# Norm products ordered by sum, the samples' last sum moved to POOL and ACT's queue, the last prompt tile finished in two column halves

## What is computed

```python
    g_, u_ = jnp.split(f @ w_gate_up, 2, axis=-1)
    x = x + rmsnorm((jax.nn.silu(g_) * u_) @ w_down, g_ffn_post)

def rmsnorm(x, g):
    x32 = x.astype(jnp.float32)
    y = x32 * lax.rsqrt(jnp.mean(x32 * x32, axis=-1, keepdims=True) + RMS_EPS)
    return (y * g.astype(jnp.float32)).astype(x.dtype)
```

## Time and profile before

| what | value |
| --- | --- |
| three runs | 806.24, 808.50, 808.62 us; median 808.5 us |
| profiled execution, its own time | 807.31 us |
| span of that execution (first to last instruction) | 805.5 us |
| PE busy | 777.1 us, 96% of the span |
| DVE busy | 472.3 us, 59% |
| ACT busy | 358.1 us, 44% |
| POOL busy | 62.4 us, 8% |
| last product of the down projection starts | 796.04 us after the span's start |
| last store started by SP | 802.93 us |
| mean granted TensorE clock | 0.987 of 2.4 GHz |

### The profile page before, as it was taken

One profiled execution on the slowest core, in us unless ns is written; L12 is line 12 of the kernel. 1 busy time (PEld: TensorE's weight loads), 2 busy tenths in 40 slices (PEclk: granted clock), 3 DMA queues, 4 the chain that ended last, 5 costly groups with the idle time before them and its releaser, 6 DMA issues.

```text
span 805.5 us, 16337 instructions
## 1 busy us (share of the span) xinstructions
PE 777.1 (96%) x6019; PEld 736.3 (91%) x6019; DVE 472.3 (59%) x739; ACT 358.1 (44%) x614; POOL 62.4 (8%) x142
## 2 busy tenths in 40 slices
PE   3999999999999999999999899999999999999996
PEld 2879998999898899996889899999999999999996
DVE  5556646636646643675558877777777776222223
ACT  6235534534534541333465455555555565222222
POOL 3321102011010110004000000000000010000000
PEclk9899999999999999999999999999999999999998
DMA  6654335335422122635443233333333224323222
GB/s 205 176 165 134 101 117 142 91 97 146 126 75 83 52 80 72 218 105 167 148 132 104 56 101 105 104 104 104 104 103 96 61 96 135 99 72 91 78 65 111
DMA packets 148746, 89.09 MB, mean 111 GB/s; under 512 B 8594, under 2 KB 142186, under 8 KB 148715
## 3 DMA queue, kind: packets, MB, share of 16 engines
q1 hardware_dynamic: 146014, 81.63, 34.4%
q0 software_dynamic: 2384, 6.40, 2.3%
q10 hardware_dynamic: 316, 0.66, 0.3%
HBM read 81.85 MB, written 6.81 MB: 110 GB/s over the span
## 4 chain that ended last, share of the span: by engine, by line
PE 91%; DVE 1%; ACT 1%; issue 1%; DVEq 0%; ACTq 0%
PE ps L843 32%; PE ps L1158 25%; PE ps L1223 17%; PE ps L1057 6%; PE ps L1127 3%; PE ps L932 1%; PE ps L945 1%; PE ps L962 1%; PE ps L1004 1%; PE ps L907 1%; PE ps L918 1%; PE ps L975 1%; PE ps L1065 0%; PE ps L1092 0%; PE ps L991 0%
## 5 line engine op out<-in xcount | busy, mean ns | idle before, releaser
L1762 DVE TENSOR_TENSOR w_lo<-w_raw,w_hi 128x1024 fp32r<-128x1024 f32 (+1 forms) x68 | 80.9, 1191 | 141.5 <-ACT w_hi L1300 141.2
L1300 ACT ACTIVATE w_hi<-w_raw 128x1024 fp32r<-128x1024 f32 (+1 forms) x68 | 70.0, 1031 | 142.2 <-PE ps L1223 82.6
L843 PE MATMUL ps<-xin_hi,w_hi 128*128 128x272 f32 x576 | 126.9, 302 | 0.0
L843 PE MATMUL ps<-xin_hi,w_lo 128*128 128x272 f32 x576 | 119.5, 289 | 0.0
L843 PE MATMUL ps<-xin_lo,w_hi 128*128 128x272 f32 x576 | 119.4, 289 | 0.0
L843 PEld LDWEIGHTS ps<-xin_hi,w_hi 128*128 128x128 f32 x576 | 90.6, 190 | 8.9 <-issue 7.6
L843 PEld LDWEIGHTS ps<-xin_lo,w_hi 128*128 128x128 f32 x576 | 91.0, 189 | 0.0
L843 PEld LDWEIGHTS ps<-xin_hi,w_lo 128*128 128x128 f32 x576 | 90.6, 190 | 0.0
L1223 PE MATMUL ps<-hid_hi,w_hi 128*128 128x272 f32 x352 | 76.0, 291 | 0.4 <-DVE hid_lo L2140 0.4
L1223 PE MATMUL ps<-hid_lo,w_hi 128*128 128x272 f32 x352 | 75.0, 287 | 0.0
L1223 PE MATMUL ps<-hid_hi,w_lo 128*128 128x272 f32 x352 | 74.9, 288 | 0.0
(11 more groups left out here) (335 smaller groups left out, 1753.5 us busy)
## 6 DMA issues: line engine op xcount, KB each, us to landing
w_raw<-in_w_in_dram SPq DMA_DIRECT2D x72, 256.0 KB, 3.2
g_raw<-in_w_gate_up_dram SPq DMA_DIRECT2D x40, 256.0 KB, 3.9
w_raw<-in_w_down_dram SPq DMA_DIRECT2D x40, 256.0 KB, 2.9
u_raw<-in_w_gate_up_dram SPq DMA_DIRECT2D x20, 256.0 KB, 3.0
e_raw<-in_w_gate_up_dram SPq DMA_DIRECT2D x20, 256.0 KB, 4.4
kc<-in_cache_k_dram SPq DMA_DIRECT2D x64, 64.0 KB, 1.9
vc<-in_cache_v_dram SPq DMA_DIRECT2D x64, 64.0 KB, 2.0
wo_raw<-in_w_out_dram SPq DMA_DIRECT2D x12, 256.0 KB, 4.0
```

The source lines that it names most:

```text
L843: mm = e.matmul(ps[:, bank + h, 0:HT], wt[:, kw, :], xt[:, kx, h * HT:h * HT + HT], start=first and wt is wh and xt is xh, stop=last and ( ...
L1300: e.activation((to or w_hi[s])[:, 0:k, :], w_raw[s][:, 0:k, :], ACT.Copy).then_inc(hi_done, count)
L1762: e.tensor_tensor(wl[:, 0:k, :], w_raw[s][:, 0:k, :], wh[:, 0:k, :].bitcast(F32), ALU.subtract).then_inc(lo_done, count)
```

## The change

There are four parts.

1. `norm_part` takes the sums in another order. Before, each tile's `yacc` product was followed by its `ysq` product, all behind the wait for the square. Now the `yacc` products of all tiles of the half are made first, without waiting for the square, and then the wait and the `ysq` products. As several sums are open at once, they go to different PSUM banks (6 and 7, and 2 for the samples), and the second half first waits for `y_root` of the first. ACT's roots read from the new places.
2. The samples' last step moves from DVE to POOL, as two instructions (`tensor_scalar`, then `tensor_tensor`, with a semaphore `zs_done` between them). POOL waits for `y_inv` 2 and `yt_free` KD + 2, the same two that DVE waits for.
3. The samples' store moves from SP's queue to ACT's, behind `zs_done` 2, after all that ACT computes.
4. DVE and SP treat prompt tile 3 in two halves of 512 columns: two instructions and two stores of 256 KB, in place of one instruction and one store of 512 KB.

The semaphore `acc_zero` is replaced by one more count of `consts_v`.

```diff
-            for tt in range(TT + 1):
+            for tt in range(TT - 1):
                 e.wait_ge(z_done, tt + 1)
-                if tt < TT:
-                    e.dma_start(y_prompt[0, tt * P:(tt + 1) * P, :], ytok[:, tt, :]).then_inc(y_out, 16)
-                else:
-                    e.dma_start(y_sample.rearrange("b t d -> (b t) d"), ytok[0:TS, TT, :]).then_inc(y_out, 16)
+                e.dma_start(y_prompt[0, tt * P:(tt + 1) * P, :], ytok[:, tt, :]).then_inc(y_out, 16)
+            for c in range(2):
+                cols = slice(NHALF * c, NHALF * c + NHALF)
+                e.wait_ge(z_done, TT + c)
+                e.dma_start(y_prompt[0, SEQ - P:SEQ, cols], ytok[:, TT - 1, cols]).then_inc(y_out, 16)
...
-            e.wait_ge(y_out, 16 * (TT + 1))
+            e.wait_ge(y_out, 16 * (TT + 2))
...
+            e.wait_ge(x1_back, 16 * (TT + 1))
+            e.wait_ge(y_inv, 2)
+            e.wait_ge(yt_free, KD + 2)
+            e.tensor_scalar(ytok[0:TS, TT, :], ytok[0:TS, TT, :], ycol[0:TS, 8 + TT:9 + TT], None, ALU.mult).then_inc(zs_done, 1)
+            e.wait_ge(zs_done, 1)
+            e.tensor_tensor(ytok[0:TS, TT, :], ytok[0:TS, TT, :], x1tok[0:TS, TT, :], ALU.add).then_inc(zs_done, 1)
...
-            def norm_part(tts):
-                for tt in tts:
-                    rows = P if tt < TT else TS
-                    for sums in (yacc, ysq):
-                        mm = e.matmul(ps[0:rows, D_BANK[0], tt:tt + 1], y_cols(sums[:, :], tt), ones[:, 0:1],
+            def norm_part(h):
+
+                units = ((0, 6), (1, 7)) if h == 0 else ((2, 6), (3, 7), (TT, 2))
+                if h == 1:
+                    e.wait_ge(y_root, 1)
+                for sums in (yacc, ysq):
+                    if sums is ysq:
+                        e.wait_ge(y_sq_last, h + 1)
+                    for tt, bank in units:
+                        rows = P if tt < TT else TS
+                        mm = e.matmul(ps[0:rows, bank, h:h + 1], y_cols(sums[:, :], tt), ones[:, 0:1],
                                       start=sums is yacc, stop=sums is ysq)
...
             e.wait_ge(ysq_used, KD)
-            e.wait_ge(y_sq_last, 1)
-            norm_part((0, 1))
+            norm_part(0)
             half_T(0)
             down_steps(2, 1, range(DOWN_K[2]), False, True, hs=(1,)).then_inc(tile_done, 1)
-            e.wait_ge(y_sq_last, 2)
-            norm_part((2, 3, TT))
+            norm_part(1)
             half_T(1)
...
+            e.wait_ge(zs_done, 2)
+            e.dma_start(y_sample.rearrange("b t d -> (b t) d"), ytok[0:TS, TT, :]).then_inc(y_out, 16)
...
-                for tt in (0, 1) if h == 0 else (2, 3, TT):
-                    rows = slice(0, P if tt < TT else TS)
-                    e.scalar_tensor_tensor(ytok[rows, tt, :], ytok[rows, tt, :], ycol[rows, 8 + tt:9 + tt], x1tok[rows, tt, :],
-                                           ALU.mult, ALU.add).then_inc(z_done, 1)
+                for tt in (2 * h, 2 * h + 1):
+                    for cols in (slice(0, D),) if tt < 3 else (slice(0, NHALF), slice(NHALF, D)):
+                        e.scalar_tensor_tensor(ytok[:, tt, cols], ytok[:, tt, cols], ycol[:, 8 + tt:9 + tt], x1tok[:, tt, cols],
+                                               ALU.mult, ALU.add).then_inc(z_done, 1)
```

More of the change, by code:

```diff
@@ L449, in program @@
         ysq_used = sem("ysq_used")
-        acc_zero = sem("acc_zero")
         yt_ready = sem("yt_ready")
@@ L456, in program @@
         z_done = sem("z_done")
+        zs_done = sem("zs_done")
         y_out = sem("y_out")
@@ L1700, in y_roots @@
                 tts = slice(2 * h, 2 * h + 2)
-                last = e.activation(ycol[:, tts], ps[:, 6, tts], ACT.Sqrt, bias=eps_col[:, :], scale=1.0 / D)
+                last = e.activation(ycol[:, tts], ps[:, 6:8, h], ACT.Sqrt, bias=eps_col[:, :], scale=1.0 / D)
                 if h == 1:
-                    last = e.activation(ycol[0:TS, TT:TT + 1], ps[0:TS, 6, TT:TT + 1], ACT.Sqrt, bias=eps_col[0:TS, :],
+                    last = e.activation(ycol[0:TS, TT:TT + 1], ps[0:TS, 2, 1:2], ACT.Sqrt, bias=eps_col[0:TS, :],
                                         scale=1.0 / D)
@@ L2211, in _ @@
             e.wait_ge(q3_done, NS)
-            e.memset(yacc[:, :], 0.0).then_inc(acc_zero, 1)
-            e.wait_ge(acc_zero, 1)
+            e.memset(yacc[:, :], 0.0).then_inc(consts_v, 1)
+            e.wait_ge(consts_v, 4)
             def down_lo(n, odd, c):
```

## The result

The changed kernel is slower by a little. Eight runs have a median of 810.20 us (808.43 to 811.41), eight of the kernel before 807.52 (806.24 to 808.62); the ratio is 1.0037, 95% interval 1.0026 to 1.0047, so about 3.0 us (the two medians differ by 2.7). The forecast was +1.9 us and 809.8 us.

The account below looks back on a forecast made before the run. PE, busy 96% of the span, bounds the kernel, so only the end can move: norm 0.60 us earlier, but POOL's samples work behind DVE's sums gives +1.9 us on 807.9, 809.8 us; range 806.6 to 811.5.

Parts of the forecast that it names:

- DVE's first sum of half 1: Second half's final sums after the norm: DVE's first would start 0.60 us earlier, at 798.64.
- POOL's multiplication: Samples' `tensor_scalar` at the end: 1.12 us for 1024 columns, ending at 802.12 behind DVE's sums.
- Norm products: Second half's norm on PE: `yacc` products hidden ahead of the square, everything behind them 0.60 us earlier.
- Tile 3 in halves: Last prompt tile on DVE and SP: 0.61 us per further half; the prompt's path alone would end 1.0 us earlier.
- The addition: Samples' `tensor_tensor` on POOL after the multiplication: 2.47 us, ending at 804.72.
- the hop: Gap between POOL's two samples instructions: 0.13 us, from 0.08 to 0.18.
- The port: Shared SBUF port at the end: DVE's 2.50 us and POOL's 3.7 us run one behind the other.
- The end: Close of the program: samples' store lands at 806.90, the span ends 0.5 us later at 807.4.
- Rival A: Final sums: no lock between POOL and DVE, span ends 0.45 us earlier, 807.4 us; chance 0.16.
- Rival B: Final sums: POOL's addition gets the port before tile 3's second half, +2.2 to +2.5 us, 810.1 to 810.4; chance 0.18.
- Rival C: Before POOL's addition: a configuration switch costing up to 9.2 us, total 810 to 819; chance 0.04.
- D: Second half's norm: PE cannot begin `yacc` products early, all times 0.5 us later, +2.4, 810.3; chance 0.05.

Follow-up runs that it names:

- norm_only: Kernel before with only the new order of norm products in `norm_part`; timed ratio 0.9996 to the kernel before, tail 0.54 us shorter.
- dve_samples: Changed kernel with the samples' last sum back on DVE, store still on ACT's queue; ratio 0.9990 to the kernel before, 0.9996 when run again.
- one_op_gelu: Kernel before with POOL's GELU multiply-and-add (128 x 544) cut to its multiplication; traced only, that instruction took 1.57 us in place of 0.64.
- two_ops: Changed kernel with the samples' multiplication on POOL written as two operations, times the reciprocals plus 0; ratio 1.0020 to the kernel before.
- drain_probe: Kernel before plus a small POOL memset of an unused table after DVE's last sum; ratio 1.0003, tail 0.97 us longer.
- drain_last: Kernel before plus a small POOL memset that waits until all stores have landed; ratio 1.0034, 2.8 us, tail 3.11 us longer.

## Why the prediction was right or wrong

The range held the result (810.2 in 806.6 to 811.5) and the direction was right. The size was not: +3.03 us in the tail for a forecast of +1.9, and slower by more than 0.3% had only a chance of 0.30, against 0.65 for no difference. That 809.8 lay so near 810.2 is partly chance, as the base that I took was 0.4 us over the median of before. From the start of PE's last product, the forecast's steps stood and fell so:

| step | forecast | measured |
| --- | --- | --- |
| DVE's first sum of half 1 | 2.60 | 2.68 |
| POOL's multiplication done | 6.08 | 6.68 |
| POOL's addition done | 8.68 | 9.10 |
| samples' store landed | 10.86 | about 11.0 |
| end of the span | 11.36 | 12.49 |

So up to the landing of the store the errors came to no more than 0.2 us, by luck, as errors of both signs nearly cancel; the rest of the miss lies behind it.

- **Norm products**: right in mechanism, 0.52 us in place of 0.60 (shown alone by norm_only). The `yacc` products did begin beside the last down product; the `ysq` ones took 0.69 to the transposes, not 0.60.
- **Tile 3 in halves, and the prompt's path is not the end**: right. Its last store (started at 800.29, 2.0 us to land) was there 2.8 us ahead of the samples' in after, and dve_samples shows no gain from the halves.
- **POOL's multiplication**: the mis-sized term, 2.84 us for 1.12. It was priced from the nearest row of the same name, and a difference between the two, one operation for two, was not looked at: one_op_gelu and two_ops show that it makes up all of it. The addition (2.33 for 2.47) and the hop (0.09 for 0.13) were right to 0.2 us.
- **The port**: right in kind, wrong in extent. POOL waited for the first DVE sum only (over 1.28 us behind DVE's start), not for all three (2.50), and DVE lost 0.87 us. This saved 1.2 us that the forecast had counted, and hid most of the 1.7 us error in the term above. The prediction did allow that the multiplication slips in earlier, but said that the total time of the port stays the same then; it did not, 6.42 us in after against 7.87 with one behind the other. A range given for POOL's price from rows of two operations could not hold it.
- **The end**: wrong by 1.0 us, and this is the step that the prediction lacked. It took "0.5 behind the last landing" from the earlier trace rows for granted, since SP was the last there. POOL's drain is in the trace of before, at line L320, 9.3 us long from 662.2; the question "what does an engine do after its last instruction, and when was it last used" would have raised it, though not its price: that row alone would have said up to 9.3 us, not the 3.1 that drain_probe and drain_last show.
- **Rival A** (no lock) fell. **Rival B** did not occur in after, and did in two_ops. **Rival C** (a switch of POOL's configuration) fell: 0.09 us between POOL's two instructions. **D** fell.
- **Two slips that moved nothing**: the rate in the earlier trace rows also dips to 355, 328 and 246 GB/s, and the way used for the multiplication gives 2.43 for the addition, not 2.39.

What stays open: what POOL's drain waits for in its 3 us (POOL starts DMA transfers earlier in every kernel here, so no run shows the drain of a POOL that starts none), why one operation costs 2.5 times as much as two, and why DVE loses only 0.87 us beside a multiplication of 2.84.

## What to carry to other kernels

An engine that is idle at the end of a kernel is not free there: using it moves its closing drain to the end as well, and for POOL that was 3.1 us from its last operation, to be set against the time that the stores need to land. A price taken from a row of the same name holds only for the same form: compare the number of operations and operands, not the name and the columns alone. Two engines that start on the same signal and share a port should be counted by when each lets it go. That does not follow from their durations; it has to be read from a trace in which the two meet.

## What was not expected of the hardware

- A `tensor_scalar` on POOL with one operation took 1.57 us on 128 x 544 and 2.84 on 32 x 1024; with two it took 0.64 on 128 x 544, and about 1.0 behind its wait on 32 x 1024.
- POOL's closing DRAIN ended 3.1 us behind its last operation, whether this was an addition of 2.33 us or a memset of 0.20; in timed runs it cost 2.8 us (1.0023 to 1.0045).
- Beside POOL's one-operation multiplication (2.84 us alone) DVE's two-input instruction lost 0.87 us, beside the two-operation form (about 1.1 with its start-up, an estimate from two_ops) 0.86; beside POOL's addition (2.33 alone) it lost 2.08.
- The same products ahead of the end took between 794.1 and 797.2 us in executions whose instructions there are almost the same, as much as the effect that was looked for: the two traces of dve_samples differ by 2.2 us there, while their tails, counted from the last product, are 9.00 and 8.97.
